# First norm by token rows, idle products, later zeroes, four projection banks, and the first output projection by token

## The reference, cut to what matters

```python
def first_block(x, ...):
    h = _rmsnorm(x, norm_mix_w)                 # the first norm
    proj = h @ w_in                             # the projections: q, k, v, z, gates, p
    qkv = silu(causal_conv(proj[qkv]))
    q, k = l2norm(q), l2norm(k)
    o = chunk_gated_delta_rule(q, k, v, g, beta)   # holds the triangular solve
    o = _rmsnorm(o, dn_norm_w) * silu(z)
    pool_out = multiscale_pool(p, w_pool, pool_scale)
    x = x + concatenate([o, pool_out]) @ w_out  # the first output projection
    x = x + _peer(_rmsnorm(x, norm_ffn_w), w_query, sub_keys, expert_down, expert_up)
    return _rmsnorm(x, norm_final_w)
# _peer: q = xn @ w_query; scores = q . sub_keys; top 16 of 128 + 128 keys, top 16 of the 256 sums;
# softmax of these as gates; sum over the chosen of 16384 experts of gate * gelu(xn . down) * up
```

## Time and profile before

| | |
|---|---|
| median of 3 runs | 1381.72 us (1381.69 to 1383.59) |
| the profiled execution | 1383.61 us, its span 1381.8 us |
| TensorE busy | 1332.3 us, 96% of the span |
| VectorE, ScalarE, GpSimd busy | 957.1, 725.0, 495.1 us |
| mean granted clock of TensorE | 0.993 |

### The profile page before, as it was taken

The page is one execution under the profiler, slowest core; times in us unless marked ns, Lnnn a source line. Parts: engine busy times, 40 slices in busy tenths (PEclk is TensorE's granted clock), DMA queues, the critical chain, the costliest instruction groups (busy, mean ns, idle before and its releaser), DMA issues.

```text
span 1381.8 us, 25722 instructions
## 1 busy us (share of the span) xinstructions
PE 1332.3 (96%) x9029; PEld 1217.2 (88%) x9029; DVE 957.1 (69%) x1776; ACT 725.0 (52%) x1063; POOL 495.1 (36%) x275
## 2 busy tenths in 40 slices
PE   5999999999999999999999999999999999999997
PEld 5898999999999999999788888888878888999996
DVE  6758468789989557775666666666666657666665
ACT  4832445777777753333444444444464446444446
POOL 1000000678768777778778787300000000000000
PEclk9999999999999999999999999999999999999999
DMA  6980234566666665556677777666665224555552
GB/s 248 382 329 5 92 132 167 156 173 183 177 176 181 180 187 149 122 144 158 197 213 220 210 211 206 222 232 237 222 225 179 97 92 164 203 183 183 184 187 88
DMA packets 89374, 251.98 MB, mean 182 GB/s; under 512 B 41008, under 2 KB 57520, under 8 KB 62432
## 3 DMA queue, kind: packets, MB, share of 16 engines
q1 hardware_dynamic: 47424, 229.23, 47.4%
q0 software_dynamic: 41888, 21.94, 10.1%
HBM read 233.18 MB, written 17.96 MB: 182 GB/s over the span
## 4 chain that ended last, share of the span: by engine, by line
PE 59%; POOL 20%; DMA 6%; issue 6%; DVE 6%; ACT 3%; SPq 0%; DVEq 0%; ACTq 0%; POOLq 0%
POOL gates_dense L401 20%; PE ps L438 18%; PE ps L440 18%; PE ps L439 18%; DMA gates_dense<-gate,spot 3%; DMA raw<-in_wts 3%; DVE wlo L434 1%; ACT whi L421 1%; PE ps L795 1%; PE ps L712 1%; PE ps L701 0%; PE ps L710 0%; DVE h L557 0%; DVE Dm L1570 0%; DMA gd<-gates_dense 0%
## 5 line engine op out<-in xcount | busy, mean ns | idle before, releaser
L434 DVE TENSOR_TENSOR wlo<-raw,whi 128x1024 fp32r<-128x1024 f32 x412 | 503.0, 1223 | 185.4 <-ACT whi L421 176.4
L421 ACT ACTIVATE whi<-raw 128x1024 fp32r<-128x1024 f32 x412 | 434.9, 1058 | 336.2 <-PE ps L440 280.2
L438 PE MATMUL ps<-ahi,whi 128*128 128x256 f32 x1888 | 545.0, 289 | 12.7 <-DVE alo L577 5.5
L401 POOL DMA_INDIRECT gates_dense<-gate,spot x256 | 484.1, 1891 | 201.4 <-issue 92.7
L439 PE MATMUL ps<-alo,whi 128*128 128x256 f32 x1888 | 536.5, 284 | 0.0
L440 PE MATMUL ps<-ahi,wlo 128*128 128x256 f32 x1888 | 536.3, 284 | 0.0
L438 PEld LDWEIGHTS ps<-ahi,whi 128*128 128x128 f32 x1888 | 364.9, 193 | 19.7 <-issue 12.4
L439 PEld LDWEIGHTS ps<-alo,whi 128*128 128x128 f32 x1888 | 364.7, 193 | 0.9
L440 PEld LDWEIGHTS ps<-ahi,wlo 128*128 128x128 f32 x1888 | 364.3, 193 | 0.0
L438 PE MATMUL ps<-whi,phi 128*128 128x512 f32 x600 | 238.2, 397 | 3.3 <-DVE plo L1782 3.2
L440 PE MATMUL ps<-whi,plo 128*128 128x512 f32 x600 | 237.9, 396 | 0.0
(11 more groups left out here) (378 smaller groups left out, 1090.8 us busy)
## 6 DMA issues: line engine op xcount, KB each, us to landing
raw<-in_wts SPq DMA_DIRECT2D x206, 1024.0 KB
gates_dense<-pf POOLq DMA_DIRECT2D x4, 4096.0 KB, 17.4
gd<-gates_dense SPq DMA_DIRECT2D x22, 256.0 KB
gd<-gates_dense SPq DMA_DIRECT2D x10, 512.0 KB
gates_dense<-gate,spot POOLq DMA_INDIRECT x256
cst<-in_c POOLq DMA_DIRECT2D x1, 1216.0 KB, 12.6
x<-in_x_t SPq DMA_DIRECT2D x1, 1024.0 KB, 4.9
kk<-in_keys POOLq DMA_DIRECT2D x1, 1024.0 KB, 5.2
```

The source lines that it names most:

```text
L401: pl.indirect_dma_start(out=dense, out_offset=bass.IndirectOffsetOnAxis(ap=spot[:, tb, h, k:k + 1], axis=0), in_=gate[:, tb, h, k:k + 1], ...
L421: nc.scalar.activation(whi[:, j, :], raw_tile(j // 2, j % 2), ACT.Copy).then_inc(s["w_hi"], 1)
L434: nc.vector.tensor_tensor(wlo[:, j, :], raw_tile(j // 2, j % 2), whi[:, j, :].bitcast(F32), ALU.subtract).then_inc(s["w_lo"], 1)
L438: nc.tensor.matmul(out_ap, wh, xh, start=first, stop=False, skip_group_check=True)
```

## The change

1. x comes by token rows (`x_tok`), in two transfers, and stays so (`xt`); the first norm is the norm by token rows, with TensorE running 14 and 4 products of ones ahead of its transposes (`spin`).
2. The first weight tile is a transfer of its own (`raw_first`); the constants `cst` and `w_pool` wait on GpSimd for the second pair of weights.
3. The first 12 projections write to four banks in turn (`proj_bank`).
4. All zeroes are issued when the last projection has been copied out.
5. The first output projection is by token: the operand is stationary and the weights move, 12 products of 512 columns a tile, into four banks; its first tile starts ahead of the spreading of o's factors, its last two tiles are worked off bank by bank, VectorE adds each half row to `xt`, and the norm by token rows follows.
6. There are no seeds. The banks keep the output of the first output projection, the experts' up products are added to it, and VectorE adds x, loaded a second time (`x_again`), when it takes them out.
7. A permutation of the banks (`late`) from there on, so that the accumulating banks are 2 to 5.

```diff
@@ sync
-            sp.dma_start(x[:, :, :], x_t).then_inc(s["x_in"], 16)
+            sp.dma_start(xt[:, 0, :], x_tok[:, 0, :]).then_inc(s["x_in"], 16)
+            sp.dma_start(xt[:, 1, :], x_tok[:, 1, :]).then_inc(s["x_in1"], 16)
             sp.dma_start(vec[:, :], vecs).then_inc(s["vec_in"], 16)
...
+            sp.dma_start(raw[:, 0, 0:TW], wts[0][:, 0:TW]).then_inc(s["raw_first"], 16)
+            sp.dma_start(raw[:, 0, TW:], wts[0][:, TW:]).then_inc(rs[0], 16)
+            sp.dma_start(raw[:, 1, :], wts[1]).then_inc(rs[1], 16)
@@ gpsimd
+            pl.wait_ge(s["raw1"], 16)
             pl.dma_start(cst[:, :], c1[:, 0:11 * P + PG * T]).then_inc(s["c1_in"], 16)
...
+            pl.wait_ge(s["evac"], N_PROJ1)
             for part in range(4):
-                pl.wait_ge(s["evac"], 4 * part + 2)
                 pl.dma_start(rows_[:, part * n_rows:(part + 1) * n_rows, :], m3(blank, n_rows)).then_inc(s["zeroed"], 16)
...
+            pl.wait_ge(s["p_split"], KT)
+            pl.dma_start(h32_t, x_tok).then_inc(s["x_again"], 16)
@@ helpers
+        def proj_bank(u):
+            return bank((0, 1, 4, 5)[u % 4] if u < 12 else u % 2, T)
+        def late(b0, n, base=0):
+            return bank((0, 1, 6, 7, 2, 3, 4, 5)[b0], n, base)
@@ tensor
-            norm_pe(pe, 0)
+            def spin(n):
+                for _ in range(n):
+                    tm(bank(2, P), ones[:, :], ones[:, :], start=True, stop=True)
+
+            pe.wait_ge(s["ones_ready"], 1)
+            spin(14)
+            pe.wait_ge(s["ident_in"], 16)
+            pe.wait_ge(s["ya"], 1)
+            pe.wait_ge(s["yd"], 1)
+            for q in range(4):
+                turn(0, h32_t, q, (0,))
+            spin(4)
+            pe.wait_ge(s["ya"], 2)
+            for q in range(2):
+                turn(0, h32_t, q, (1,)).then_inc(s["turned"], 1)
+            pe.wait_ge(s["yd"], 2)
+            for q in range(2, 4):
+                turn(0, h32_t, q, (1,)).then_inc(s["turned"], 1)
...
             for u in range(N_PROJ1):
                 pe.wait_ge(s["w_lo"], u + 1)
-                if u >= 2:
-                    pe.wait_ge(s["evac"], u - 1)
-                gemm_tile(pe, u % RING, bank(u % 2, T), 0 if u == 0 else None)
+                if u >= 4:
+                    pe.wait_ge(s["evac"], u - (3 if u < 12 else 1))
+                gemm_tile(pe, u % RING, proj_bank(u), 0 if u == 0 else None)
...
+            token_rows(4, 0, ahi[:, 4, :], alo[:, 4, :], (1, 2, 3), first=True)
             pe.wait_ge(s["o_rn"], 1)
+            pe.wait_ge(s["mix_pool"], 1)
             for i in range(NI):
-                m = along_row(bank(4, P, base=i * P), col["o_r"][:, i:i + 1])
+                m = along_row(bank(0, P, base=i * P), col["o_r"][:, i:i + 1])
...
-            for n in range(KT):
-                gemm_tile(pe, n % RING, bank(n % 2, T), 1 if n == 0 else None)
-            seed(0)
-            seed(2)
-            square_sum(pe, 1)
-            seed(1)
-            norm_row(pe, 1)
-            seed(3).then_inc(s["seeded"], 1)
+            token_rows(4, 0, ahi[:, 4, :], alo[:, 4, :], (0,), first=True).then_inc(s["w_used"], 1)
+            for n in range(1, KT - 2):
+                k = (n + 4) % KT
+                pe.wait_ge(s["w_lo"], W_OUT1 + n + 1)
+                pe.wait_ge(s["operand"], 4 + n // 2 + 1)
+                token_rows(4, n % RING, ahi[:, k, :], alo[:, k, :]).then_inc(s["w_used"], 1)
+            pe.wait_ge(s["w_lo"], W_QUERY)
+            pe.wait_ge(s["operand"], 8)
+            for b0 in range(4):
+                for n in (KT - 2, KT - 1):
+                    m = token_rows(4, n % RING, ahi[:, n - 4, :], alo[:, n - 4, :], (b0,))
+                if b0 < 3:
+                    m.then_inc(s["x_ps"], 1)
+            m.then_inc(s["w_used"], 2)
@@ scalar, the first norm (the second is the same with x1 in place of x_in)
+            act.wait_ge(s["x_in"], 16)
+            row_squares(0, 0, xt[:, 0, :], sq_t[:, 0, :])
+            act.wait_ge(s["t_sq"], 1)
+            row_root(0, 0, 0, eps)
+            act.wait_ge(s["x_in1"], 16)
+            row_squares(0, 2, half_row(xt, 3), half_row(sq_t, 3))
+            act.wait_ge(s["t_r"], 1)
+            A(half_row(h32_t, 0), half_row(xt, 0), ACT.Copy, scale=r_col[:, 0, 0:1]).then_inc(s["ya"], 1)
...
+            split_hi(act, 0, 0)
+            act.wait_ge(s["t_r"], 2)
+            A(half_row(h32_t, 2), half_row(xt, 2), ACT.Copy, scale=r_col[:, 0, 1:2]).then_inc(s["ya"], 1)
+            act.wait_ge(s["vec_in"], 16)
+            for q in range(4):
+                turned_act(act, 0, q, mix_weight)
@@ vector, end of the first output projection
+                    for b0 in range(3):
+                        dve.wait_ge(s["x_ps"], b0 + 1)
+                        x_rows(b0)
+                    row_inverse(1, 0, 3)
...
+                    dve.wait_ge(s["w_used"], W_QUERY)
+                    x_rows(3)
...
+                    for q in range(2):
+                        turned_dve(dve, 2, q, peer_weight)
                 lo_for(W_OUT1 + n)
+            for q in range(2, 4):
+                turned_dve(dve, 2, q, peer_weight)
@@ vector, after the experts
-            V.tensor_copy(half_row(xt, b0), bank(4 + b0, 512)).then_inc(s["xd"], 1)
+                V.tensor_tensor(half_row(xt, b0), half_row(h32_t, b0), late(4 + b0, 512), ALU.add).then_inc(s["xd"], 1)
```

516 lines of the change are left out of this document (239 added, 277 removed).

## The result

On record were 5 executions of each kernel: the changed one 1374.6 us median (1372.98 to 1376.96), the one before 1381.72 (1381.31 to 1383.59).

A forecast was written before the change was run, and what follows sets the result against it. TensorE bounds the expert stages, so the first 192 us decide. 5.2 + 4.7 + 4.2 = 14.1 us off the profiled 1383.61 gives 1369.5; as a median, 1.9 lower, 1367.5 us, range 1362.5 to 1373.5.

The forecast's parts named there:

- rival of the clock: Clock falls again behind waits before the gates and norms, or in the second norm: two falls of 1.7, 1371 us; chance 0.15.
- What bounds the kernel: Both expert stages are bound by TensorE, so whatever the first 192 us give or lose arrives at the end unchanged.
- First term, -5.2: First norm by rows and idle products: small transposes at 25.0 instead of 30.3, -5.2 us (-3.5 to -6.5).
- The first product follows at 5.7 + 5.5 = 11.2: Start: x's second half lands at about 5.7, the norm takes 5.5, so the first projection product starts at 11.2 us.
- 15.2 + 4.83 + 0.8 + 4.1: Start: reload issue, its trip, 0.8 for constants under way, then 4.1 to the small transposes, giving 25.0 us.
- What they bring, a first tile at full clock, is worth nothing: Idle products at the start: 0, as VectorE's quarters pace the first tile and the reload bounds what follows.
- Second term, -4.7: Projections with later zeroes: 1.2 to the norms, 1.8 at the wait at 82.04, 1.7 of clock fall; range -1.2 to -7.6.
- The zeroes' new place: Zeroes start at about 95 us, take 41 us at 405 GB/s, and end at 136, before the solve ends at 141.
- Four banks, 0: Projections: both bank waits, 1.41 and 1.48 us, go, but TensorE then waits for gates and norms; 0, at most -2.9.
- Third term, -4.2: Output projection by token and the second norm, up to the first query tile: -4.2 us (-2.0 to -5.5).
- a slow start is absorbed by the same wait: Output projection: the clock's second fall (154.44) matters little, as the wait for the last two tiles' weights absorbs it.
- x read again later: Second read of x, named beside the removed seeds in the third term, with no size given.

The follow-up runs named there:

- copy_first: Changed kernel with the first norm's second scaled copy ahead of tile 0's split on ScalarE, without the 4 idle products: 1376.03 us, ratio 0.9944 to the kernel before.
- copy_idle: Changed kernel with the second scaled copy ahead of the split, 18 idle products first and 10 behind the second transposes: 1376.05 us, ratio 0.9953.
- start_all: copy_idle with the constants asked for only when the first reload of weights has landed: 1370.55 us, ratio 0.9910 to the kernel before.
- idle_more: Changed kernel with 18 and 10 idle products instead of 14 and 4, and 5 more behind the second transposes: 1375.9 us, ratio 0.9946.
- two_banks: Changed kernel with the projections over two banks again instead of four: 1374.07 us, ratio 0.9926 to the kernel before.
- rows_first: Changed kernel with the broadcast of the output norm's row ahead of the nine early products of the output projection: 1375.72 us, ratio 0.9939.
- cst_only: Changed kernel with only the request for the constants moved behind the landing of the first reload: 1375.33 us, ratio 0.9953.
- zero_old: Changed kernel with the gate table's zeroes back in four parts inside the projections: 1378.78 us, ratio 0.9967 to the kernel before.
- x_by_sp: Changed kernel with x's second read issued by SyncE in the weights' queue, behind the last reload of the experts' second stage: 1373.25 us, ratio 0.9938.
- start_again: start_all executed once more, on the chip of the changed kernel's repeat: 1370.96 us, ratio 0.9919 to the kernel before.
- before_zero_late: Kernel before the change with only its zeroes moved behind the last projection: 1379.6 us, ratio 0.9978.
- final: best with x's second read issued by SyncE in the weights' queue instead of in four pieces: 1367.66 us, ratio 0.9893 to the kernel before.
- warm_kept: start_again plus idle products in TensorE's idle pieces where a bank is free: 1369.61 us, ratio 0.9910 to the kernel before.
- best: warm_kept with vec behind the first weights, the operand's first quarter ahead of the split, x's second read in four pieces: 1371.51 us, ratio 0.9924.
- no_idle: Changed kernel without its 14 + 4 idle products ahead of the first norm: 1375.47 us, ratio 0.9952 to the kernel before.

## Why the prediction was wrong, step by step

**What bounds the kernel: right.** The experts' stages kept their length, and from the first query tile to the end it is 1190.9 us against 1189.4. The 1.5 us are the longer fall of the clock in the attention (63.8 us against 62.3), which the prediction's rival of the clock did not look for so late.

**First term, -5.2: this step failed; measured -1.9** (28.44 against 30.31). It was the mis-sized term, 3.3 us of the 5.1 by which the landmarks miss. In the profile on record the reload goes out at 17.96 instead of 15.2 (2.8 later) and takes 5.14 instead of 5.6; with the 4.13 behind it the transposes could have come at 27.2, and TensorE, slow in the first tile, arrives 1.2 later still. Three parts of it:
- "The first product follows at 5.7 + 5.5 = 11.2": x's second half was there at 6.3, and the weights of tile 0 at 10.16, past the 9.5 of the bound. The prediction had put the copy behind them on ScalarE into the bound, not into the sum. With the copy ahead the first product came at 13.1 to 13.5, not 11.2: the split and the subtraction of tile 0 (1.06 and 1.22) follow the landing in any order.
- "15.2 + 4.83 + 0.8 + 4.1": the 4.1 held (4.13 in 16 of the 20 profiles, the one on record not among them). The reload's trip, 4.83 + 0.8 in the sum, was 5.14 in the first profile and 6.3 to 6.4 in the five others with the same start, with constants and an instruction read in it. copy_first, copy_idle and start_all show that it was the last wait in these variants: 1.2 us earlier products changed nothing until the constants were out of the way, and then 2.15 came.
- "What they bring, a first tile at full clock, is worth nothing": right while the reload bounds (idle_more, two_banks, rows_first: full clock, transposes at 28.15 to 28.50). In the profile on record, in which the reload landed early, at 23.10, the slow 5.7 us of products were the limit, and in cst_only, zero_old and x_by_sp they and the reload (plus 4.13) ended within 0.2 us of each other. So it is the last wait that says what a clock is worth, and with this start two waits are nearly level: removing one alone shows little.
With the three removed the transposes stand at 25.43 to 26.15 in six profiles, 4.2 to 4.9 us ahead of the kernel before: most of the 5.2 were there, and the change as made collects a third of them.

**Second term, -4.7: right, measured -5.0**, and by its parts: small transposes to the norms' rows 43.27 to 42.03 us, -1.2 (1.2 forecast); rows to the normed keys' products 8.46 to 6.47, -2.0 (1.8); from there to the transposes of the solve's matrix 14.83 to 13.06, -1.8 (1.7, the fall that had stood there). A fall came at 64.52 instead, against the forecast, and cost nothing by luck of its place: it filled the idle 1.27 us that runs without it show ahead of the norms' rows (start_all at 67.75), and the stretch is 42.0 us with it and without. Falls elsewhere in the stretch do cost: with one at 28.6 to 29.5 the stretch is 43.5 us (copy_idle, rows_first), with 10.2 us at the lower level 44.9 to 45.1 (idle_more, copy_first, start_again). before_zero_late gives the same 4.8 alone.

**The zeroes' new place: right in the result, not in the margin.** The mixed rate was taken, 405 GB/s; they moved 373 and landed at 146.7, 2.9 us behind the solve instead of 5 ahead of it. Nothing wanted the engines until the keys, asked for at 154.7, and the next reload at 156.1. The keys shared the engines with that reload (1.05 MB of the 2.66 MB moved from 153 to 163 us), but they did so before, too (159.2 and 160.5). The reload's weights came 19.0 us behind the last sum of squares instead of 17.6. The zeroes are not the cause, for zero_old, with them in the projections, has the same 19.0 (166.76). It was asked for 12.5 us behind that sum instead of 10.1, and 1.9 of the 2.4 is the broadcast (4.7 behind it, 2.8 before), which now stands behind nine products; the forecast had 0.6 for it. Whether this sets the stage's end is open: rows_first had the weights 17.4 behind the sum and ended no earlier.

**Four banks, 0: right**, 0.1 us.

**Third term, -4.2: measured -3.6** (solve to first query tile 83.21 to 79.57). Both executions have two falls of the clock in it; without any it is 77.7 and 78.0 in copy_idle and two_banks, 1.6 to 1.9 less. So "a slow start is absorbed by the same wait" was probably wrong by up to that. It is not clean: the four kernels with idle products there have no falls either and take 77.7 to 80.0, and the two longest of these (final, warm_kept) have the longest waits of ScalarE for those weights among the four, 7.04 us.

**"x read again later", priced by silence at 0: wrong in 7 of the 15 profiles with the read on GpSimd in one piece**, 0.9 to 1.4 us between starts (0.23 is the pace). The profile on record was one without it. The prediction names the read and gives it neither a term nor a rival. The Trainium skill, "DMA: Bandwidth & Descriptors", section "Issuing engines are not separate DMA queues", has it that transfers of all issuing engines run on the same engines and interleave. The traces agree as far as they go: in best three of the four pieces on GpSimd's queue have a late reload and a wait of TensorE 9.4 to 9.9 us behind them, and when the read stood in the weights' queue (x_by_sp, final) no wait followed it. The fourth wait in best comes 16.5 us behind its piece, and for it the link is not shown.

**The rival of the clock** came true in its mechanism, with falls behind the waits for the norms and in the second norm, as it said, and two more; at 1371 it was 3.6 us short, since the start's miss is not in it.

**Profiled execution and median.** The kernel before was profiled 1.9 us over its median, the changed one at its own. Hence 9.0 between the spans and 7.1 between the medians; the ratio, 0.9941, stands for 8.2, and 0.9937 on the second chip for 8.7.

## What to carry to other kernels

When a stall is removed at the start, follow the chain to the next transfer that the freed work asks for, and list everything that crosses the DMA engines during that trip: here a megabyte reload and a slow first tile were nearly level, and an earlier first product alone gained nothing, 1.5 MB of constants moved behind the reload alone gained nothing, and the two together, with more idle products, some 2 us. A clock that falls costs only where TensorE is last; fill idle pieces when a bank is free (gains of 1.35 us in the median here, inside the noise), but first look at what waits behind them. A read that "has time" should be tried in the queue of the transfers it must not disturb: two profiles with it there are clean, though 8 of 15 without are too.

## What the runs showed of the hardware

- The 1 MB reload at the start, with nothing but the next reload beside it, took 4.76 to 4.94 us from issue to use in 8 executions; with other transfers inside the trip, 5.14 to 7.41. With one instruction read of 16 KB as the only other, 6.30 and 6.35; that the read is the cause was not tested.
- The granted clock fell behind an idle piece in some executions and not in others at the same place: ahead of the gates' product (1.60 us idle) it fell in start_again, at 40.8, and not in start_all or no_idle; in the attention (1.6 us idle) it fell in 15 of the 16 profiles without idle products there, and not in no_idle. With idle products in these pieces it held for some 1360 us in three kernels.
- What one fall of 3.4 us costs where TensorE sets the pace: 1.1 us in the attention (61.2 us without a fall in 5 profiles, 62.2 to 62.3 with one in 14, 63.8 with one of 6.8 us), 1.8 behind the normed keys (14.83 us before, 13.08 in before_zero_late), nothing ahead of a wait. That is not the whole spread of executions: the changed kernel's five spans lie 4.0 us apart, warm_kept's, with the clock at 0.997 to 0.999, 5.0.
